# A two-layer transformer front, a gated delta block and 16 experts on one core: the second chunk stream's decay matrices made within the first stream's levels

## The reference, cut to what matters

```python
gcum = jnp.cumsum(chunks(g), axis=-1)
diff = gcum[..., :, None] - gcum[..., None, :]
decay = jnp.where(tri, jnp.exp(jnp.where(tri, diff, 0.0)), 0.0)
a_mat = jnp.where(strict, jnp.einsum("nbhid,nbhjd->nbhij", kb, kc) * decay, 0.0)
t_inv = lax.linalg.triangular_solve(eye + a_mat, eye, left_side=True, lower=True, unit_diagonal=True)
u = t_inv @ (vc * bc[..., None])
w = t_inv @ (kb * jnp.exp(gcum)[..., None])
attn = jnp.einsum("nbhid,nbhjd->nbhij", qc, kc) * decay
def step(state, xs):
    v_new = u_i - w_i @ state
    o_i = q_i @ state + a_i @ v_new
    state = state * jnp.exp(gl_i)[..., None, None] + jnp.swapaxes(k_i, -1, -2) @ v_new
    return state, o_i
```

## Time and profile before

| what | us |
|---|---|
| median of 3 runs (1196.56 to 1196.95) | 1196.66 |
| profiled execution | 1202.21 |
| its span | 1200.4 |
| TensorE busy | 1018.7 (85%) |
| VectorE busy | 428.3 (36%) |
| ScalarE busy | 237.5 (20%) |
| GpSimd busy | 54.3 (5%) |

### The profile page before, as it was taken

One profiled execution on the slowest core, in us unless ns is written; L12 is line 12 of the kernel. 1 busy time (PEld: TensorE's weight loads), 2 busy tenths in 40 slices (PEclk: granted clock), 3 DMA queues, 4 the chain that ended last, 5 costly groups with the idle time before them and its releaser, 6 DMA issues.

```text
span 1200.4 us, 18176 instructions
## 1 busy us (share of the span) xinstructions
PE 1018.7 (85%) x7714; PEld 530.7 (44%) x7714; DVE 428.3 (36%) x1021; ACT 237.5 (20%) x589; POOL 54.3 (5%) x70
## 2 busy tenths in 40 slices
PE   5999999999999989999998889998656766666666
PEld 2344764444477446886567765432111111111111
DVE  0137746333765527445247782411100000000002
ACT  0011135011213423444113352200000000000002
POOL 0101000000100000000222400000000000000000
PEclk9999989999999999999998999998898899788889
DMA  9973238543325994013132026999999999999996
GB/s 384 403 281 141 97 126 338 186 185 141 140 79 219 429 387 166 1 71 141 72 142 73 4 72 252 415 421 430 429 430 431 429 429 430 431 429 427 433 429 264
DMA packets 28160, 323.69 MB, mean 270 GB/s; under 512 B 3264, under 2 KB 3392, under 8 KB 5808
## 3 DMA queue, kind: packets, MB, share of 16 engines
q1 hardware_dynamic: 26048, 314.18, 63.9%
q0 software_dynamic: 2032, 8.35, 1.9%
HBM read 321.47 MB, written 1.05 MB: 269 GB/s over the span
## 4 chain that ended last, share of the span: by engine, by line
PE 60%; DMA 31%; DVE 4%; issue 2%; ACT 1%; SPq 1%; DVEq 0%; ACTq 0%
PE banks L650 49%; DMA zuv_to_Kt<-in_stream 17%; DMA ring<-in_stream 14%; PE banks L661 3%; PE banks L2207 1%; PE banks L922 1%; PE banks L908 1%; PE banks L943 1%; SPq L555 1%; PE banks L905 1%; PE banks L800 1%; DVE KC L1259 0%; PE banks L913 0%; PE banks L946 0%; DVE probs L1309 0%
## 5 line engine op out<-in xcount | busy, mean ns | idle before, releaser
L650 PE MATMUL banks<-ring,uT 128*128 128x512 f32 (+1 forms) x512 | 228.1, 600 | 7.2 <-DMA ring<-in_stream 4.2
L650 PEld LDWEIGHTS banks<-ring,uT 128*128 128x128 f32 x512 | 96.9, 193 | 122.7 <-issue 113.6
L650 PE MATMUL banks<-ring,scr_qk 128*32 128x512 f32 (+1 forms) x496 | 82.6, 621 | 28.6 <-DMA ring<-in_stream 28.0
L650 PE MATMUL banks<-scr_qk 64*64 64x64 f32 (+2 forms) x2368 | 84.6, 267 | 23.4 <-DMA scr_qk<-in_stream 19.1
L2773 DVE SCALAR_TENSOR_TENSOR UWK<-UWK,banks 128x256 f32<-128x256 f32 x16 | 6.7, 421 | 265.8 <-ACT UWK L3055 265.8
L650 PE MATMUL banks<-ring,UWK 128*32 128x512 f32 (+1 forms) x336 | 85.7, 788 | 13.3 <-ACT UWK L3063 7.0
L3055 ACT ACTIVATE UWK<-banks 128x256 f32<-128x256 f32 x16 | 6.1, 383 | 362.6 <-PE banks L650 362.6
L650 PEld LDWEIGHTS banks<-scr_qk 64*64 64x64 f32 (+2 forms) x2368 | 55.9, 134 | 46.9 <-issue 35.0
L650 PE MATMUL banks<-UWK,ring 128*128 128x256 f32 x320 | 71.0, 380 | 0.0
L2207 PE MATMUL banks<-UWK 128*128 128x512 f32 x128 | 65.1, 632 | 0.9 <-DVE UWK L2781 0.9
L650 PEld LDWEIGHTS banks<-UWK,ring 128*128 128x128 f32 x320 | 60.4, 190 | 9.3 <-issue 1.4
(11 more groups left out here) (383 smaller groups left out, 1208.5 us busy)
## 6 DMA issues: line engine op xcount, KB each, us to landing
ring<-in_stream SPq DMA_DIRECT2D x93, 2048.0 KB, 14.5
scr_qk<-in_stream SPq DMA_DIRECT2D x11, 2048.0 KB, 39.1
Vt_to_O<-in_stream SPq DMA_DIRECT2D x11, 2048.0 KB, 38.8
zuv_to_Kt<-in_stream SPq DMA_DIRECT2D x10, 2048.0 KB, 39.1
scr_qk<-in_stream SPq DMA_DIRECT2D x11, 1024.0 KB, 41.4
wide<-in_stream SPq DMA_DIRECT2D x10, 1024.0 KB, 38.1
const<-in_stream SPq DMA_DIRECT2D x10, 1024.0 KB, 36.9
misc<-in_stream SPq DMA_DIRECT2D x10, 1024.0 KB, 39.7
```

The lines of the kernel that those rows point to most:

```text
L650: return pe.matmul(o, a, b, start=start, stop=stop)
```

## The change

1. `spread`, `R_mm`, `diff`, `decay` and the product with beta of stream 1 are made inside stream 0's levels, in the area of `attnT` instead of `scr`: on VectorE the spread after level 0, the difference of tile n-1 after levels 1 and 2, beta after level 4; on TensorE `R_mm` of tile n-1 after levels 1 and 2, in banks 4 and 0; on ScalarE the exponentials after level 4's copies. At stream 1's head, VectorE waits only for `beta_decay`, for `W_mm` of stream 0 and for `G_mm`.
2. The mask of level 1 (GpSimd) waits for `M` of level 0 instead of for level 0's `Y_mm` and `TT`.
3. Three refills of the ring wait for more than before (`quiet`): the one behind `zuv_mm` 2 for `Z_mm` of stream 0, level 1; the one behind `zuv_mm` 1 for `Z_mm` of level 3; the one behind `zuv_mm` 0 for stream 1's last `W_mm`. The next unit, the first into the key area, is issued behind the third.

```diff
+        quiet = {("zuv_mm", 2, 1): ("Z_mm", 0, 1, 1), ("zuv_mm", 1, 1): ("Z_mm", 0, 1, 3),
+                 ("zuv_mm", 0, 1): ("W_mm", 1, 1, 1)}
...
                 elif before[k] is not None:
                     sp.wait_ge(*at(*units[before[k]]))
+                    if units[before[k]] in quiet:
+                        sp.wait_ge(*at(*quiet[units[before[k]]]))
...
         def pool_M(pool, s, n, t):
-            pool.wait_ge(*at("Y_mm", s, t, n - 1))
             if n == 1:
-                pool.wait_ge(*at("TT", s, t, 0))
+                pool.wait_ge(*at("M", s, t, 0))
+            else:
+                pool.wait_ge(*at("Y_mm", s, t, n - 1))
...
+        def pe_R(pe, s, t):
+            b = R_bank(s, t)
+            pe.wait_ge(*at("spread", s, t))
+            pe.wait_ge(*free(b))
+            mm(pe, bank[b][:, :], C("same"), spread_at(s, t), True, True).then_inc(*fill(b, "R_mm", s, t))
...
-            for t in range(TILES):
-                pe.wait_ge(*at("spread", s, t))
-                pe.wait_ge(*free(4 * t + 2))
-                mm(pe, bank[4 * t + 2][:, :], C("same"), scr[:, t, T_, :], True, True).then_inc(...)
+            if s == 0:
+                for t in range(TILES):
+                    pe_R(pe, s, t)
...
                 if s and n <= 3:
                     pe_ctx_KV(pe, n)
+                if s == 0 and 1 <= n <= 2:
+                    pe_R(pe, 1, n - 1)
                 if s == 0 and 1 <= n <= 4:
                     pe_zuv(pe, zw, (1, 1, 0, 0)[n - 1], (n - 1) % 2, 4 * ((n - 1) % 2))
...
+        def spread_at(s, t):
+            return attnT[:, t, :, :].rearrange("p i n -> p (i n)") if s else scr[:, t, T_, :]
+        def decay_at(s, t):
+            return attnT[:, t, :, :].rearrange("p i n -> p (i n)") if s else scr[:, t, M_, :]
...
+        def R_bank(s, t):
+            return 4 - 4 * t if s else 4 * t + 2
+        def v_diff(dve, s, t):
...
+        def v_beta(dve, s, t):
...
             for t in range(TILES):
...
+                b = 4 * t
+                if s == 0:
+                    v_beta(dve, s, t)
+                else:
+                    dve.wait_ge(*at("beta_decay", s, t))
+                    dve.wait_ge(*at("W_mm", 0, t, 1))
                 dve.wait_ge(*at("G_mm", s, t))
...
         def v_chunks(dve, s):
-            if s:
-                for t in range(TILES):
-                    v_spread(dve, 1, t)
...
+                if s == 0 and n == 0:
+                    for t in range(TILES):
+                        v_spread(dve, 1, t)
+                if s == 0 and 1 <= n <= 2:
+                    v_diff(dve, 1, n - 1)
+                if s == 0 and n == 4:
+                    for t in range(TILES):
+                        v_beta(dve, 1, t)
...
+        def a_decays(act, s):
+            for t in range(TILES):
+                act.wait_ge(*at("diff", s, t))
+                act.activation(decay_at(s, t), decay_at(s, t), ACT.Exp).then_inc(*tick("scalar_step", "decay", s, t))
...
+                if s == 0 and n == 4:
+                    a_decays(act, 1)
```

More of the change, by code:

```diff
@@ L2447, in four @@
             }[order]()
+        def spread_at(s, t):
+            return attnT[:, t, :, :].rearrange("p i n -> p (i n)") if s else scr[:, t, T_, :]
+        def decay_at(s, t):
+            return attnT[:, t, :, :].rearrange("p i n -> p (i n)") if s else scr[:, t, M_, :]
         def v_spread(dve, s, t):
             g = TILES * s + t
-            if s:
-                dve.wait_ge(*at("W_mm", 0, t, 1))
-            dve.tensor_tensor(four(scr[:, t, T_, :], "all"), four(C("tri64"), "dir"),
+            dve.tensor_tensor(four(spread_at(s, t), "all"), four(C("tri64"), "dir"),
                               four(gg[:, g, :], "each"), ALU.mult).then_inc(*tick("vector_step", "spread", s, t))
+        def R_bank(s, t):
+            return 4 - 4 * t if s else 4 * t + 2
+        def v_diff(dve, s, t):
+            b, g, dt = R_bank(s, t), TILES * s + t, decay_at(s, t)
+            dve.wait_ge(*at("R_mm", s, t))
+            dve.tensor_tensor(dt.rearrange("p (i n) -> p i n", i=NDH),
+                              bank[b][:, :].rearrange("p (i n) -> p i n", i=NDH),
+                              over(gc[:, g, :], CH), ALU.subtract).then_inc(*drain(b))
+            dve.wait_ge(*drained(b))
+            dve.tensor_tensor(four(dt, "all"), four(dt, "all"), four(C("neg64"), "dir"), ALU.add).then_inc(*tick("vector_step", "diff", s, t))
+        def v_beta(dve, s, t):
+            dt = decay_at(s, t)
+            dve.wait_ge(*at("decay", s, t))
+            dve.tensor_tensor(four(dt, "all"), four(dt, "all"), four(beta[:, TILES * s + t, :], "each"), ALU.mult).then_inc(*tick("vector_step", "beta_decay", s, t))
+            dve.wait_ge(*last("vector_step"))
         def v_head(dve, s):
@@ L2461, in v_head @@
                                   None, ALU.mult).then_inc(*drain(4 * t + 1, "Vt", s, t))
+            if s == 0:
+                for t in range(TILES):
+                    v_diff(dve, s, t)
             for t in range(TILES):
[L2463 to L2470, removed]
-            for t in range(TILES):
-                b, g = 4 * t, TILES * s + t
-                dve.wait_ge(*at("decay", s, t))
-                dt, aT_ = scr[:, t, M_, :], scr[:, t, AT_, :]
-                dve.tensor_tensor(four(dt, "all"), four(dt, "all"), four(beta[:, g, :], "each"), ALU.mult).then_inc(*tick("vector_step"))
-                dve.wait_ge(*last("vector_step"))
+                b = 4 * t
+                if s == 0:
+                    v_beta(dve, s, t)
+                else:
+                    dve.wait_ge(*at("beta_decay", s, t))
+                    dve.wait_ge(*at("W_mm", 0, t, 1))
                 dve.wait_ge(*at("G_mm", s, t))
+                dt, aT_ = decay_at(s, t), scr[:, t, AT_, :]
                 ins = dve.tensor_tensor(four(aT_, "all"), four(bank[b][:, 0:256], "head"), four(dt, "all"), ALU.mult)
@@ L2490, in v_head @@
                     dve.tensor_tensor(attnT[:, t, :, :].rearrange("p (r h) i -> p r h i", r=2), four(bank[b][:, 256:512], "head"),
-                                      four(scr[:, t, M_, :], "all"), ALU.mult).then_inc(*drain(b))
+                                      four(decay_at(s, t), "all"), ALU.mult).then_inc(*drain(b))
                     dve.wait_ge(*drained(b))
@@ L2931, in a_chunks @@
                 act.activation(Kt[:, t, :, :].rearrange("p h d -> p (h d)"), bank[4 * t][:, :], ACT.Copy).then_inc(*drain(4 * t, "Kt", s, t))
-            for t in range(TILES):
-                act.wait_ge(*at("diff", s, t))
-                act.activation(scr[:, t, M_, :], scr[:, t, M_, :], ACT.Exp).then_inc(*tick("scalar_step", "decay", s, t))
             if s == 0:
+                a_decays(act, 0)
                 a_norm_exp(act, "l", 2 * H2, "lat_norm")
```

1 line of the change is left out of this document (removed).

## The result

The changed kernel takes 1191.3 us, median of 11 runs (1187.67 to 1195.71), against 1196.66 for the kernel before on the same chip: a ratio of 0.9947, 95% interval 0.9931 to 0.9963, so 6.3 us of 1196.66 (4.4 to 8.3); the two medians themselves are 5.4 us apart. 1190.4 was forecast.

A forecast was written before the change was run, and what follows sets the result against it. DMA was taken to bound the kernel from about 740 us to the end, TensorE the chunk streams before. Stream 0's 0.0, the head's 3.4 and 2.9 to `WS` sum to 6.3 us: 1196.66 to 1190.4 us, range 1187.3 to 1194.3.

The forecast's parts named there:

- mask of level 1, stream 0: Level 1 of stream 0: the earlier mask lets TensorE start sooner; gain 1.9 us, bounds 1.5 and 3.3.
- two `R_mm` in stream 0: Products moved from stream 1's head into stream 0, where TensorE has no gap to hide them; loss 1.88 us.
- boundary at level 4's end: Four added pairs move an instruction block boundary from inside the large product to level 4's end; loss 0.95 us.
- gap in `U_mm`: Stream 0: without a refill under way the instruction block arrives before it is needed; gain 0.96 us, bounds 0 and 0.96.
- stream 0 in sum: Mask, `R_mm`, boundary and `U_mm` terms together: 0.0 us, bounds given as -2.4 to +2.4.
- transposes to level 0: Stream 1's head: `G_mm` follows the transposes at once, so level 0 starts earlier; gain 3.4 us.
- level 0 to first `WS`: Stream 1: VectorE sets `WS`'s start, 6.65 us after level 0's; gain 2.9 us, nearly all from avoiding the half clock.
- Hold-back: Refills delayed past fetch-sensitive parts of stream 0; only the 0.96 us stall in `U_mm` counted as gain.
- Hidden fetch: Rival: block boundaries cost nothing once the refills are gone; gain 8.65 us, 1188.0 us; chance 0.18.
- The clock did not fall: Rival denied here: TensorE's clock falls again in stream 1, losing the 2.9 us; gain 3.4, 1193.3 us; chance 0.14.
- the decay was not what the head waited for: Rival: something else holds stream 1's level 0, gap and half clock stay; gain 1.9, 1194.8 us; chance 0.10.
- Two refills in a row: Rival: refills issued together at about 681 us starve an engine of instructions; 5.8 us slower, 1202.5 us; chance 0.03.

The follow-up runs named there:

- e2: Changed kernel with the old waits of the level masks: median 1195.02 us, ratio to the kernel before 0.9960 to 0.9998.
- e5: Changed kernel plus 58 small products (116 load-and-matmul pairs) in the second layer at about 425 us: median 1191.17 us, ratio to the kernel before 0.9961.
- e10: Changed kernel plus 37 small products (74 pairs) at TensorE's very beginning: median 1192.25 us, ratio to the kernel before 0.9944 to 0.9978.
- e6: Changed kernel plus 63 small products (126 pairs) in the second layer at about 425 us: median 1196.28 us, ratio to the kernel before 0.9988.
- e9: Changed kernel plus 58 small products (116 pairs) at TensorE's very beginning: median 1191.76 us, ratio to the kernel before 0.9938 to 0.9970.
- e3: Kernel before plus the new mask wait (stream 0 only) and held-back refills, no decays moved: median 1195.01 us, ratio to the kernel before 0.9976.
- e1: Changed kernel with its three refills not held back: median 1195.55 us, ratio to the kernel before 0.9983.
- e4: Changed kernel with old mask waits and refills not held back, so the decays' move alone: median 1195.07 us, ratio to the kernel before 0.9982.
- e8: Changed kernel with one more VectorE mask step at stream 1's head: median 1190.35 us, ratio to the kernel before 0.9937, from 6 runs.
- e7: Changed kernel with three more VectorE mask steps at stream 1's head: median 1193.86 us, ratio to the kernel before 0.9956 to 0.9987.

## Why the prediction was right

By its own steps, with the profiled executions of before and after:

| term | predicted | measured |
|---|---|---|
| mask of level 1, stream 0 | +1.9 | +1.76 |
| two `R_mm` in stream 0 | -1.88 | -1.93 |
| boundary at level 4's end | -0.95 | -1.02 |
| gap in `U_mm` | +0.96 | +1.17 |
| level 3 without a refill | not named | +0.40 |
| stream 0 in sum | 0.0 | +0.60 |
| transposes to level 0 | +3.4 | +3.31 |
| level 0 to first `WS` | +2.9 | +2.75 |
| recurrence | 0 | 0.01 |
| in sum | 6.3 | 6.67 |

*Level 1.* It ended 8.04 us after level 0's start, where it was 9.80; its boundary stayed where it was, and its gap of 1.30 too, as written. e2 gave the term back with 2.03. The five terms of stream 0 that the table measures add up to 0.38; of the 0.22 left, 0.20 lie in the two large products behind an `R_mm`, which take 6.96 and 6.97 us from start to start where it was 7.07 and 7.06. So the two `R_mm` really cost 1.73.

*`R_mm`.* They take 0.97 and 0.96 us (577.35 to 578.32, 589.16 to 590.12). Not all of the moved work lies within the large products: VectorE's spreads run beside level 1 (from 573.17), ScalarE's table load and exponentials over the end of level 4 (610.78 to 613.2). e5 and e10 have the same work at the same places and no gap there, so it cost TensorE nothing that the rows show.

*Boundaries.* e5, e6, e9 and e10 show that the gaps belong to a place in the code with a period of about 126 pairs, and to nothing that an engine does there: 116 or 74 pairs more take them from levels 1 and 4, 126 bring them back. The forecast that the four pairs of `R_mm` bring the gap before the large product, and in full, held (1.34 us for 0.48; in e3, with the refills held back but without the four pairs, the gap is still inside it, 0.29). Loss 1.02: level 4 with its product is 12.61 us, before 11.59. What rests on an argument still is that these gaps are instruction fetch, and that a block is asked for at the start of the one before it; no run shows the request.

*Hold-back.* `U_mm` gained a little more than said. The step that was undersized is the one that counted only this gap, although it was forecast with bounds of 0 and 0.96: e1 puts the whole hold-back at 2.87 us in stream 0, since with the other parts made, the refill would fall on level 1's boundary. Level 3, which ran 4.28 us with a refill over it and 3.88 without, was missing in the sum. Two readings in this step were off without changing the term: the refill issued at 623.19 took 8.8 us, and not the median of 7.7; and the bounds given for stream 0 add up to -1.5 and +2.4, not -2.4.

*Head.* e4 and e8 show the mechanism and the size. In the chain of waits of the kernel after, VectorE holds all from `G_mm` to `WS`, as forecast: 0.72 us gap before level 0 (said 0.6) and 0.20 before `WS` (said 0.7).

*Level 0 to `WS`.* 2.75 of 2.9, but of two causes. I laid nearly all of it to the half clock. e2 and e4, with the full clock and the old mask, have 7.48: the clock and what goes with it gave 2.07, and the mask of stream 1 0.68, which the prediction did not have at all. In the 2.07 lies also a step of VectorE, the second tile's product with beta (0.68 us at 642.75), which stood in this stage and is gone from it; no run parts it from the clock. That the sum of the stage came out so close is owed to reckoning VectorE's chain, which does bind it; the split was wrong.

*The rivals.* Hidden fetch (the rule of the Trainium skill, "Runtime: NRT & Kernel Launch", "Instruction fetch mechanics", that a crossing is mostly hidden) does not hold for this code, if the gaps are fetch: those of 1.30 and 1.34 stand with no refill beside them. It holds for e10's alignment in stream 0. The clock did not fall after 0.72 us; e7 shows that it can after 2.90, and the price of a fall is between its 0.72 us (3.4 us at half clock) and at most the 2.07 of the kernel before (6.8 us), not 2.9. That the decay was not what the head waited for is refuted by B (4.75 in e4, with the decays alone). Two refills in a row starved nothing: though 4 MB move from 679 us on, the whole latent recurrence keeps its length. From its first `WS` (569.31 + 61.94 + 4.75 + 6.80 + 37.42 = 680.22) to the product behind it in this row it is 24.75 us, and before, by the same sum, 689.91 to 714.67, 24.76:

```profile
704.97 10.54 PE L656 MATMUL banks<-ring,scr_qk 128*128 128x512 f32 x24 [0.34 <-ACT scr_qk L3034]
```


*The end.* The gain at the end of D is 9.7 us between the two profiles, and 10.9 at the end of the span; 3.0 and 1.2 of these lie where nothing was changed. That the 6.67 us of the stages reach the end whole fits the runs (6.3, 4.4 to 8.3), but they can't show it to a microsecond.

The forecast of the time was 0.9 us low. With single runs 8 us apart and an interval of about 4 us for the gain, the runs can't tell such small terms. The stages show those of the head and of level 0 to `WS`, and that `U_mm`'s gap is gone wherever the refills are held back. For the terms of level 1 and level 4, and for the sum of stream 0 (+0.60 where 0.0 was said), profiles of one program differ by about a microsecond: that they agree with the forecast to a tenth or two is in part luck.

## What to carry to other kernels

When a wait of one engine is taken away, look at what else falls due just there: the hold-back was worth 2.87 us with the other parts made, and the decays alone gave less than a third of the whole (2.03 of 6.67). In a long run of small products, one load to one matmul, a gap of about a microsecond can belong to a place in the code, most likely because they run faster than their instructions are fetched; then instructions added earlier move it, and large transfers should not run over it. Compare stages that end on the same event, and take two profiles of one kernel before believing a difference of about a microsecond.

## What was not expected of the hardware

VectorE and GpSimd slow each other down. VectorE's spread took 0.64 us before; beside GpSimd's mask, in the kernel after (the timelines of the two engines), each took 1.44:

```profile
573.17 2.88 DVE L2472 TENSOR_TENSOR Vt_to_O<-const,lows 128x512 f32<-128x512 f32 x2
...
575.98 0.67 DVE L2543 TENSOR_TENSOR scr_qk<-scr_qk,banks 128x512 f32<-128x512 f32 x1
```

```profile
561.01 2.00 POOL L583 TENSOR_TENSOR scr_qk<-scr_qk,const 128x512 f32<-128x512 f32 x1 [0.63 <-DVE scr_qk L2519]
572.91 2.59 POOL L583 TENSOR_TENSOR scr_qk<-scr_qk,const 128x512 f32<-128x512 f32 x2 [9.90 <-PE banks L656]
```

GpSimd's mask took 2.00 us at 561.01 beside VectorE, 1.07 (2.14 for two) elsewhere. A step of VectorE that reads PSUM keeps its length beside GpSimd (L2512 at 635.82 took 0.68 us). The Trainium skill, "GPSIMD Engine Reference", Specifications, tells of such a contention between the two for access to SBUF, for VectorE's instructions with two operands there; the rows agree. Beside this mask it cost nothing, as TensorE was in level 1. In e2 and e4 the spreads fall on the masks that TensorE waits for, and it stands idle 0.35 us for the second; and one such step, L2519 at 636.53 (1.08 us), is in the chain at stream 1's head, and is a part of its length.

The clock is not a function of the gap alone. Behind 1.50 us idle before level 1 it stayed at its full level (2.4 GHz) in the kernel before and went to half (1.2 GHz) in e2 and e4, where the second gap of 0.35 us stands close behind it; behind 1.45 us it stayed in e8; behind 2.31 (e3), 2.32 (before) and 2.90 us (e7) it fell, for about 6.8, 6.8 and 3.4 us. But it also stayed behind 1.88 us in e4's `U_mm` and behind the 2.63 us of e1 in level 1, longer than two of the gaps behind which it fell. Two windows of e1, in that gap and after it:

```profile
573.00:574.00 1.00, 0.00 (x0) 0.00 (x0) 1.00 (x2) 0.00 (x0) 0.00 (x0) 1.00 0.07 16
...
576.00:577.00 1.00, 1.00 (x4) 0.41 (x3) 1.00 (x3) 0.00 (x0) 0.00 (x0) 1.00 0.07 16
```

The Trainium skill, "TensorE: Matmul & The Clock Gate", Part 1, has the activity window run freely; that like gaps have unlike outcomes agrees with that, but no run here shows the window.
